# A decoder layer on one core: the second output gate's weights between cached key units, the sample state product in column quarters

## The reference

```
mod = dot(silu(c), w_ada) + b_ada                    # 6 x 1024 columns: shift, scale and gate, twice
z   = (rmsnorm(x) * (1 + sc1) + sh1) @ w_in          # q,f,i,g of HGRN2 | q,k,v of MoBA | two output gates
S   = diag(f_t) S + (1 - f_t) outer i_t;  o_t = S^T q_t          # prompt: from 0; sample: from state_hgrn
att = softmax over (3 best past blocks, own block) of q.k, times v   # sample: 2048 cached keys per sequence
y   = sigmoid(ga) * (o @ w_proj_a) + sigmoid(gb) * (att @ w_proj_b)
x1  = x + gate1 * rmsnorm(y @ w_out)
out = x1 + gate2 * rmsnorm(swiglu(...w_gu) @ w_down)
```

## Time and profile before

| what | value |
|---|---|
| median of 3 runs | 765.85 us (760.8 to 769.72) |
| the run that was profiled | 767.38 us, of which the span of the instructions is 765.5 us |
| PE, DVE, ACT, POOL busy | 657.4, 413.2, 273.8, 77.2 us |
| 0 to 131 us | start, conditioning, w0 to w7 or so |
| 131 to 172.8 us | last input weights w8 to w13 with ada pairs |
| 172.8 to 276.5 us | cached keys |
| 276.5 to 308 us | w14 to w17, choice of blocks |
| 308 to 456.6 us | values with w18 to w21, recurrence, prompt attention |
| 456.6 to 765.5 us | the later dense layers |

### The profile page before, as it was taken

How to read it: one execution, slowest core, us unless ns; L and a number is a source line. 1 busy time by engine, 2 the same in 40 slices (tenths; PEclk the granted TensorE clock), 3 DMA queues, 4 the chain that set the end, 5 groups by cost and what they waited for, 6 DMA issues and landing times.

```text
span 765.5 us, 13144 instructions
## 1 busy us (share of the span) xinstructions
PE 657.4 (86%) x5251; PEld 552.0 (72%) x5251; DVE 413.2 (54%) x493; ACT 273.8 (36%) x390; POOL 77.2 (10%) x86
## 2 busy tenths in 40 slices
PE   4759999986867769889967759985999999999996
PEld 1237999774655559768423329984999999999996
DVE  0641479357999979320387325767635353543522
ACT  1232435253221136223312223353645454532421
POOL 2040005101364000000000000004200000000001
PEclk9859999997999699997668959998999999999987
DMA  8895952978999978896565998540464546445201
GB/s 334 318 349 209 357 186 87 353 252 290 351 332 307 336 287 230 290 324 203 188 210 157 325 343 274 184 148 0 124 188 153 172 143 190 150 151 182 87 1 62
DMA packets 96305, 168.93 MB, mean 221 GB/s; under 512 B 6449, under 2 KB 37865, under 8 KB 93058
## 3 DMA queue, kind: packets, MB, share of 16 engines
q1 hardware_dynamic: 90386, 162.85, 62.7%
q10 hardware_dynamic: 5152, 3.08, 1.4%
q0 software_dynamic: 720, 2.32, 0.8%
HBM read 163.51 MB, written 4.72 MB: 220 GB/s over the span
## 4 chain that ended last, share of the span: by engine, by line
PE 66%; DVE 12%; DMA 9%; POOL 4%; SPq 4%; issue 3%; ACT 2%; POOLq 0%; DVEq 0%; ACTq 0%
PE ps L1399 17%; PE ps L1401 16%; PE ps L1400 16%; DMA ring<-w_in 6%; DVE KT L1060 4%; SPq L302 2%; DMA ring<-w_ada 2%; PE ps L1565 2%; PE ps L1410 2%; POOL hx L475 2%; PE ps L1598 2%; PE ps L1630 2%; PE ps L1546 2%; PE ps L1762 1%; DVE wl_lo L906 1%
## 5 line engine op out<-in xcount | busy, mean ns | idle before, releaser
L897 DVE TENSOR_TENSOR w_lo<-ring,w_hi 128x1024 fp32r<-128x1024 f32 (+1 forms) x112 | 133.4, 1218 | 124.9 <-ACT w_hi L540 124.8
L1399 PE MATMUL ps<-h_hi,w_hi 128*128 128x288 f32 x576 | 174.1, 302 | 14.4 <-POOL h_lo L436 9.5
L1400 PE MATMUL ps<-h_lo,w_hi 128*128 128x288 f32 x576 | 172.0, 299 | 0.0
L1401 PE MATMUL ps<-h_hi,w_lo 128*128 128x288 f32 x576 | 171.3, 297 | 0.0
L540 ACT ACTIVATE w_hi<-ring 128x1024 fp32r<-128x1024 f32 (+1 forms) x112 | 113.8, 1040 | 153.7 <-PE ps L1401 87.1
L1399 PEld LDWEIGHTS ps<-h_hi,w_hi 128*128 128x128 f32 x576 | 109.9, 191 | 22.5 <-issue 13.1
L1401 PEld LDWEIGHTS ps<-h_hi,w_lo 128*128 128x128 f32 x576 | 110.4, 192 | 0.0
L1400 PEld LDWEIGHTS ps<-h_lo,w_hi 128*128 128x128 f32 x576 | 110.3, 191 | 0.1
L1060 DVE STREAM_TRANSPOSE KT<-ring 128x2048 f32<-128x2048 f32 x32 | 72.3, 2286 | 9.1 <-PE ps L1546 5.7
L1546 PE MATMUL ps<-KT,Wk 128*32 128x128 f32 x1024 | 39.4, 303 | 21.4 <-DVE KT L1060 21.4
L1546 PEld LDWEIGHTS ps<-KT,Wk 128*32 128x32 f32 x1024 | 29.8, 120 | 32.9 <-DVE KT L1060 23.3
(11 more groups left out here) (314 smaller groups left out, 1004.7 us busy)
## 6 DMA issues: line engine op xcount, KB each, us to landing
ring<-cache_k SPq DMA_DIRECT2D x128, 256.0 KB, 4.0
ring<-cache_v SPq DMA_DIRECT2D x128, 256.0 KB, 3.6
ring<-w_ada SPq DMA_DIRECT2D x24, 1024.0 KB, 7.5
ring<-w_in SPq DMA_DIRECT2D x22, 1024.0 KB, 7.8
ring<-w_gu SPq DMA_DIRECT2D x44, 512.0 KB, 4.7
ring<-w_down SPq DMA_DIRECT2D x10, 1024.0 KB, 5.0
ring<-w_out SPq DMA_DIRECT2D x4, 1024.0 KB, 5.4
S<-state_hgrn SPq DMA_DIRECT2D x4, 512.0 KB, 7.3
```

Source lines behind the costliest of these rows:

```text
L897: dve.tensor_tensor(w_lo[:, par, k, :], slot4(s)[:, k, :], w_hi[:, par, k, :].bitcast(F32), ALU.subtract).then_inc(sem("lo_split"), 1)
L1399: pe.matmul(dst, h, x_hi, start=first, stop=False)
L1400: pe.matmul(dst, h, x_lo, start=False, stop=False)
L1401: return pe.matmul(dst, l, x_hi, start=False, stop=last)
```

## The change

It moves the weights of the second output gate (8 column tiles). They were w18 to w21, four slots of 512 rows by 512 columns, loaded between values; they become `WK`, w14 to w17, four slots of 1024 rows by 256 columns, which enter the ring behind keys 5, 11, 17 and 23. Each is split in two halves: ACT `hi_k`, DVE `lo_k` (at units 6 and 8, 12 and 14, 18 and 20, 24 and 26), PE `dense_k` (24 matmuls each, after units 6, 9, 12, ... 27), with buffers of their own. The first gate's slots become w18 to w21 (`WL`): three of them stand directly behind the keys, the fourth behind value 1. The intra-chunk products use one pair of PSUM banks in place of two, `keep` moves by a unit, and POOL's preparations are interleaved another way. The last eight ada slots are spread behind w7 to w12 in place of pairs ahead of w10 to w13, and the small turns around them move. The sample state product becomes `sample_reads`, 8 matmuls whose 32 output rows are one of four row quarters and whose 512 columns are 4 sequences, a masking multiply on DVE (`xm`, 128x1024), and 8 matmuls with the identity that add up and turn it. `after` is laid out anew: the recurrence starts at value 4, the prompt steps at every second value from 10 to 28.

```diff
@@ -249,28 +253,32 @@
...
-    GROUPS = [4, 5, 6, 1, 0, 2, 3, 7, 8, 9, 10]
+    GROUPS = [4, 5, 6, 1, 0, 2, 3]
     NF = 7
+    WK, WL = range(14, 18), range(18, 22)
...
     RING = [("ada", k) for k in range(DT)]
     a = iter(range(DT, 3 * DT))
-    for w in range(2 * NF):
-        if w in (0, 2, 3, 4) or w >= 10:
-            RING += [("ada", next(a)), ("ada", next(a))]
-        RING.append(("in", w))
+    ADA_AFTER = {-1: 2, 1: 2, 2: 2, 3: 2, 7: 1, 8: 1, 9: 1, 10: 1, 11: 2, 12: 2}
+    for w in range(-1, 2 * NF):
+        if w >= 0:
+            RING.append(("in", w))
+        RING += [("ada", next(a)) for _ in range(ADA_AFTER.get(w, 0))]
     NA = len(RING)
-    RING += [("key", u) for u in range(NKU)]
-    RING += [("in", w) for w in range(14, 18)]
-    for w in range(18, 22):
-        RING += [("value", 2 * (w - 18)), ("value", 2 * (w - 18) + 1), ("in", w)]
-    RING += [("value", v) for v in range(8, NVU)]
+    for u in range(NKU):
+        RING.append(("key", u))
+        if u in (5, 11, 17, 23):
+            RING.append(("in", WK[u // 6]))
+    NB_ = len(RING)
+    RING += [("in", w) for w in WL[:3]] + [("value", 0), ("value", 1), ("in", WL[3])]
+    RING += [("value", v) for v in range(2, NVU)]
...
@@ -328,7 +339,12 @@
...
-                sp.dma_start(slot4(n % NSLOT), w_src("w_in", w % 2 * BK * P, GROUPS[w // 2] * BC)).then_inc(sem(f"w_landed{n % NSLOT}"), 16)
+                if w in WK:
+                    i = w - WK[0]
+                    sp.dma_start(slot8(n % NSLOT), w_src("w_in", 0, 9 * BC + 256 * i, rows=D, width=256)).then_inc(sem(f"w_landed{n % NSLOT}"), 16)
+                else:
+                    g = GROUPS[w // 2] if w < 2 * NF else 7 + (w - WL[0]) // 2
+                    sp.dma_start(slot4(n % NSLOT), w_src("w_in", w % 2 * BK * P, g * BC)).then_inc(sem(f"w_landed{n % NSLOT}"), 16)
...
@@ -343,25 +359,19 @@
...
-            for j in range(4):
-                pages = page_numbers(SPE, 4 * j, 4)
-                slot_free(NA + j)
-                load_pages(sp, "cache_k", pages, (NA + j) % NSLOT)
-            with sp.Fori(1, NSEQ) as b:
-                for j in range(4):
-                    pages = page_numbers(SPE, b * NPG + 4 * j, 4)
-                    sp.wait_ge(sem("key_slots"), b * 4 + (j - 3))
-                    load_pages(sp, "cache_k", pages, (NA + j) % NSLOT)
-
-            for n in range(NA + NKU, N_OF["value", 16]):
+            for n in range(NA, N_OF["value", 16]):
                 kind, i = RING[n]
                 if kind == "in":
                     load_in(n)
+                elif kind == "key":
+                    pages = page_numbers(SPE, 4 * i, 4)
+                    slot_free(n)
+                    load_pages(sp, "cache_k", pages, n % NSLOT)
                 else:
                     pages = page_numbers(SPE, i, 4, NPG)
                     slot_free(n)
                     load_pages(sp, "cache_v", pages, n % NSLOT)
-                if i == 1:
...
@@ -548,11 +572,29 @@
...
+                act.wait_ge(sem("w_used"), max(w * 2 + (half - 1), 2 * WL[0]))
                 k = slice(2 * half, 2 * half + 2)
...
+
+            def hi_k(w, half):
+
+                n = N_OF["in", w]
+                if half == 0:
+                    act.wait_ge(sem(f"w_landed{n % NSLOT}"), 16 * in_slot(n))
+                act.wait_ge(sem("w_used"), w * 2 + half)
+                act.activation(wk_hi[:, :, :], slot8(n % NSLOT)[:, 4 * half:4 * half + 4, :], ACT.Copy).then_inc(sem("hi_split"), 1)
+
+            def evac_k(w):
+
+                i = w - WK[0]
+                for j in range(2):
+                    if j == 0:
+                        act.wait_ge(sem("tile_done"), 3 * NF + i + 1)
+                    else:
+                        act.wait_ge(sem("w_used"), 2 * w + 2)
+                    act.activation(proj[:, bass.ds(UB + 2 * i + j, 1), :], ps[:, 4 + j:5 + j, 0:T], ACT.Copy).then_inc(sem("tile_out"), 1)
...
@@ -1032,32 +1082,43 @@
...
             def turn_keys(u):
 
-                s = (NA + u) % NSLOT
-                dve.wait_ge(sem(f"page_landed{s}"), 64 * in_slot(NA + u))
-                if u >= 2:
+                n = N_OF["key", u]
+                s = n % NSLOT
+                dve.wait_ge(sem(f"page_landed{s}"), 64 * in_slot(n))
+                if u < 2:
+                    dve.wait_ge(sem("w_used"), 4 * NF - 2 + 2 * u)
+                else:
                     dve.wait_ge(sem("kt_used"), u - 1)
                 dve.transpose(KT[:, u % 2, :, :], ring[:, s, :].rearrange("p (g n) -> p g n", n=512)).then_inc(sem("key_slots"), 1)
+
+            def lo_k(w, half):
+
+                dve.wait_ge(sem("hi_split"), w * 2 + (half + 1))
+                dve.tensor_tensor(wk_lo[:, :, :], slot8(N_OF["in", w] % NSLOT)[:, 4 * half:4 * half + 4, :], wk_hi[:, :, :].bitcast(F32), ALU.subtract)\
+                    .then_inc(sem("lo_split"), 1)
...
@@ -1080,7 +1141,7 @@
...
-                b0 = 2 + 2 * (gi % 2)
+                b0 = 2
...
@@ -1100,12 +1160,14 @@
...
-                if u % 2 == 1 and 7 <= u < 23:
-                    keep((u - 7) // 2)
-
-            lo_late(14, 0)
+                if u % 2 == 0 and 6 <= u < 22:
+                    keep((u - 6) // 2)
+                if u % 6 in (0, 2) and 6 <= u < 30:
+                    lo_k(14 + (u - 6) // 6, u % 6 // 2)
+
+            lo_late(18, 0)
             block_sums(NSEQ - 1)
-            lo_late(14, 1)
+            lo_late(18, 1)
...
@@ -1192,9 +1254,8 @@
...
-            for w in range(18, 22):
-                lo_late(w, 0)
-                lo_late(w, 1)
+            dve.wait_ge(sem("ds_done"), 1)
+            dve.tensor_tensor(xm[:, :, :], ps[:, 2:4, :].rearrange("p t (b e) -> p (t b) e", e=DK), over(C("seq"), 2, DK), ALU.mult).then_inc(sem("vm_ready"), 1)
             sample_state(0)
...
@@ -1464,13 +1525,39 @@
...
+            def dense_k(w, half):
+
+                i = w - WK[0]
+                pe.wait_ge(sem("lo_split"), w * 2 + (half + 1))
+                if half == 0:
+                    pe.wait_ge(sem("tile_out"), 4 * NF + 2 * i)
+                for j in range(2):
+                    for kt in range(4):
+                        c = slice(j * P, j * P + P)
+                        ins = three(ps[:, 4 + j, 0:T], (wk_hi[:, kt, c], wk_lo[:, kt, c]), h_hi[:, 4 * half + kt, :], h_lo[:, 4 * half + kt, :],
+                                    half == 0 and kt == 0, half == 1 and kt == 3)
+                    if j == 1:
+                        ins.then_inc(sem("w_used"), 1)
+                    elif half == 1:
+                        ins.then_inc(sem("tile_done"), 1)
+
+            ada_n = iter(range(DT, 3 * DT))
+
+            def ada_after(w):
+                for _ in range(ADA_AFTER.get(w, 0)):
+                    i = next(ada_n)
+                    ada(i // DT, i % DT)
...
@@ -1511,31 +1592,31 @@
...
+            dense_in(8)
...
-            dense_in(9)
...
+            dense_in(9)
+            pe.wait_ge(sem("q_spread"), 1)
+            pe.wait_ge(sem("own_out"), 1)
+            to_tokens(AK, "k_turned_tok")
             for w in range(10, 14):
-                ada_pair(2 * w - 4)
                 dense_in(w)
...
@@ -1590,12 +1672,12 @@
...
-                if gi >= 2:
-                    pe.wait_ge(sem("kept"), gi - 1)
+                if gi >= 1:
+                    pe.wait_ge(sem("kept"), gi)
...
@@ -1621,18 +1703,25 @@
...
-            def hgrn_sample_out(h):
+            def sample_reads():
 
                 pe.wait_ge(sem("s0_landed"), 64)
-                pe.matmul(ps[:, 6, h * TSA:(h + 1) * TSA], hvs[:, h, :], hAs[:, h, :], start=True, stop=False, skip_group_check=True)
+                for g in range(2):
+                    for h in range(HH):
+                        ins = pe.matmul(ps[32 * h:32 * h + 32, 2 + g, :], hqt[:, h, SAMP], S0[:, 4 * g:4 * g + 4, h, :], start=True, stop=True)
+                ins.then_inc(sem("ds_done"), 1)
+
+            def hgrn_sample_out():
+
+                pe.wait_ge(sem("vm_ready"), 2)
                 for b in range(NSEQ):
-                    c = h * TSA + b * TS
-                    ins = pe.matmul(ps[:, 6, c:c + TS], S0[:, b, h, :], hqt[:, h, TP + b * TS:TP + (b + 1) * TS], start=False, stop=b == NSEQ - 1, skip_group_check=True)
-                if h == HH - 1:
-                    ins.then_inc(sem("o_done"), 1)
+                    pe.matmul(ps[:, 6, 0:P], xm[:, b, :], ident, start=b == 0, stop=False, skip_group_check=True)
+                for h in range(HH):
+                    ins = pe.matmul(ps[:, 6, h * TSA:(h + 1) * TSA], hvs[:, h, :], hAs[:, h, :], start=False, stop=h == HH - 1, skip_group_check=True)
+                ins.then_inc(sem("o_done"), 1)
...
@@ -1690,9 +1779,12 @@
...
-            between = {1: [lambda: turn_ada(2)], 3: [turn_hgrn], 23: [hgrn_states]}
+            turn_ada(2)
+            between = {1: [turn_hgrn], 23: [hgrn_states]}
             for gi in range(8):
```

(47 more changed lines are left out.)

186 lines of the change are left out of this document (96 added, 90 removed).

## The result

The change makes the kernel slower by a little under 1%: 771.09 us (median of 20 runs, 768.19 to 778.95) against 765.45 us (20 runs, 760.8 to 771.1), a ratio of 1.0084 with the 95% interval [1.0063, 1.0106]. The profiled execution has a span of 767.8 us against 765.5. One execution of the kernel of experiment 7 took 1517 us, twice as long as its others, and is left out of its numbers.

What follows compares the result with a forecast made beforehand. The key stage was taken as bound by the DMA feed, DVE close behind; PE bound the late weights and early values. Terms -3 + 47 - 49 gave 762.4 us, slow restarts 3 more, forecast 765 us, range 746 to 784.

Steps and rivals of the forecast that it cites:

- part B: Key stage: the ring runs empty once per WK slot, released by the second `lo_k`; 151 against 103.7 us, +47 (+41 to +56).
- signs named: New profile: key-stage DMA share near 0.8, four SP waits, PE and DVE idle 5 to 6 us, periods 30 to 34 us.
- Ahead of the first stand nine units, 9 x 3.24 = 29, plus both lower parts, 31: Key stage, start to the first moved slot's release: nine units at feed pace and two lower parts, 31 us.
- three such periods are 96: Key stage, between releases: listed steps 30.5 or 29.3 us plus 1 to 3 for gram waits, taken as 32 each.
- the last five units: Key stage behind the last release: 5.5 + 4 x 3.15 + about 6 for the last unit's work, 24 us.
- The 3 us for slow restarts: Behind the four key-stage drains: PE's slow restart, priced at half of 1.5 us each, raises the total to 765.4.
- Rival 2: Key stage: drains keep PE at its lower clock, delaying every period to 34.5 to 36 us; +10, about 777; chance 0.22.
- Part A: Last input weights, 131 to 172.8 us: spreading the ada slots removes PE waiting and slow clock; 3 us less, bounds 0 to 5.7.
- Rival 3: Key stage: slots load between units at no drain, +13 or less there; -39 in total, about 726; chance 0.04.
- Part C: Last key to 456.6 us: three weights ahead of value 0, values at feed pace; 131 against 180.1 us, -49 (-53 to -42).
- I take 4 in all: Value stage, PE: the products replacing the 64 four-column ones, plus identity and small products, take 4 us.
- The 14 us that the old products were priced at: Value stage, PE: the 64 four-column products at 0.22 us each, from 3.58 us for 16, take 14 us away.

Runs made afterwards that it cites:

- experiment 7: Kernel before the change, with only the sample state product in column quarters, its mask and its order taken over: 749.49 us, ratio 0.9824 to the kernel before.
- experiment 1: Changed kernel, but ACT copies each moved slot's second half out, and SP waits for that copy and the first lower part: 739.42 us.
- experiment 2: Changed kernel with ACT's copies of the second halves, but SP waits for the second lower part again: 770.57 us, ratio 1.0078 to the kernel before.
- experiment 8: Changed kernel with ACT's copies and early slot release, plus `keep` a unit later: 733.66 us, ratio 0.9563 to the kernel before.
- experiment 3: Changed kernel with DVE's second lower part ahead of `keep` instead of behind it: 759.5 us, ratio 0.9942 to the kernel before.
- experiment 4: Changed kernel with `keep` moved a unit later, slot release left as it is: 759.05 us, ratio 0.994 to the kernel before.
- warm6: Changed kernel with 20 unread matmuls on PE ahead of each of the four first dense halves: 776.03 us, ratio 1.0131 to the kernel before.
- Experiment 5: Changed kernel with 56 unread matmuls on PE behind units 8, 14, 20 and 26: 772.29 us; a second variant puts fillers ahead of the first halves.
- Experiment 6: Changed kernel with the last eight ada slots in pairs ahead of w10 to w13 again: 774.71 us, ratio 1.0147 to the kernel before.

## Why the prediction missed

The forecast was 765 us with 746 to 784 as the range. The measured 771.09 lies inside, but the sign is the other one: 2 us less was forecast, 5.6 more came. The mechanism named in part B is the one that the runs show, and the miss is in its size: the wait of `keep` for a gram ahead of the first release, a term that the sum had at nothing.

- **Part B, the mechanism: right.** The release behind the second lower part sets the feed. Experiments 1 and 2 show it: one wait, moved and moved back, is worth 31 us each way. Of the signs named, SP's four waits, DVE's idle time of 5.6 to 6.3 us at the four places and value 0 at its time came; PE stood still longer than the 5 to 6 us (8.9 to 10.0), and the DMA share fell further, to 0.70 for 0.8. The rival in which the words hold (no drain) did not come; experiment 8 shows what it would have needed.
- **Part B, "Ahead of the first stand nine units, 9 x 3.24 = 29, plus both lower parts, 31": this step failed.** It measured 35.8. The 29 were right, 28.4 us to the end of unit 8's transpose, and that is luck: w14's own MB was left out of the count (the wait of 3.40 at 188.23), and unit 0, which was turned ahead of the stage, was counted in. What failed is the rest. Behind unit 8 the sum had one lower part, 1.2 us; measured are 7.4: `keep`'s wait of 4.17 for a gram, 1.3 for `keep`, and a lower part of 2.0 in place of 1.2. The sum gave grams their 1 to 3 us only in the periods, and the order rows showed `keep` ahead of this lower part too. With the lower part ahead of `keep` the release comes at 31.8, with `keep` a unit later at 30.2 (experiments 3 and 4), so the 31 would have been right without that wait. About half of it goes when PE is kept at its higher clock ahead of the first half (warm6, 33.3).
- **Part B, "three such periods are 96": right in sum, 97.2,** though two of them, 35.9 and 28.8, lie outside the 30 to 34 that was named as the sign. Without the gram waits they are 91.1 (experiment 3), so the listed steps, 30.5 + 29.3 + 29.3 = 89.1, were good to 2 us and the gram waits cost 6 in the three periods.
- **Part B, the last five units: 25.7 for 24.** The upper bound of the part, 160, holds one slow restart; with one in each period, as its text says, it is 163. The measured 158.7 lies inside either way.
- **The 3 us for slow restarts** were added to the sum as a term of their own. Experiment 5 shows that behind the holes they cost nothing; ahead of the first half the lower clock cost 2 us once and 1 once. Rival 2's mechanism, the clock entering each period behind its hole, is refuted by warm, and warm6 leaves 3 us of it in all; its sizes (a period of 35 us, +56) came close for another reason in the main, the order of keep and the lower part.
- **Part A: about right**, -2.4 for -3, in two executions that can differ by more than that up to here (172.8 and 168.8 us with the same code). Experiment 6 gives the spread 2 us.
- **Rival 3's total** of 726 leaves out the 1.9 us around the span; its own terms give 728. It did not come.
- **Part C: right**, -47.4 for -49. Value 0 came at 24.1 for 24.5. The step "I take 4 in all" for the new products measured 5.0. The 14 us that the old products were priced at come from a row at the lower clock (3.58 us for 16; the first 16 took 1.95, see below), so the price held their slowness, but not that of their neighbours. The trace of quarter shows 13.0 us from the sample product alone, in a stage where PE was the bound. In the changed kernel the value stage runs at the feed (DMA share 0.94), as forecast. How much of the 47.4 belongs to the moved gate and how much to the sample product there was not measured. But the sample product alone makes the kernel before 13 us faster, so the rest of the change (the moved gate, the earlier `keep`) cost some 20 us (ratios 1.0084 and 0.9824) if the two add up, which no run tests.

In one line: the sum missed 5 us in the key stage (beyond the 3 for restarts) and 1.6 in part C, against an expected net of -2. With two terms near 50 of opposite sign, 5 us decide the sign, and the chances (0.28, 0.44, 0.28) said no more than that.

The Trainium skill, "DMA: Bandwidth & Descriptors", section "Rules for kernel authors", which says to issue early and wait late, was set against the order rows in the prediction. The runs agree with the rule once its condition is met: the load is early only if the slot that it blocks is given back early (stash_keep, 733.66 us), and with the release late the same order of loads costs 32 us (771.09 against 739.42, `keep` early) or 25 (759.05 against 733.66, `keep` late).

## What to carry to other kernels

In a ring that one queue fills in order, ask of every entry not when its data is needed but when its slot is given back, and who is the next entry in that slot. An entry with a long hold stops everything behind its successor; copying its data out can be worth several times its price (here four copies of 1.05 us on an engine with room bought 31.7 us). When you add up the time to a release, go through every instruction ahead of it on its engine and ask what each waits for; put the instruction that releases a slot ahead of any instruction that waits for another engine.
